# Opening stage of a two-block kernel: filter sizes summed on VectorE, the modulation bias added as columns, filter products on both halves of the array, the next stage's first operands requested early

## The reference, cut to what matters

```
sh1, sc1, gt1, sh2, sc2, gt2 = split(silu_c @ ada_w + ada_b, 6)
hid  = sin(freq * (feats @ w1 + b1))
hid  = sin(freq * (hid @ w2 + b2))
filt = (hid @ w3) * exp(-t * deltas)
filt = filt / sum(abs(filt), axis=0)
return filt[:, :512], filt[:, 512:]
```

## Time and profile before

| | us |
|---|---|
| median of three runs (4322.47 to 4328.15) | 4327.37 |
| the profiled execution, its own time | 4322.88 |
| its span in the trace | 4321.1 |
| first stage, from the start to ScalarE's last instruction | 121.5 |
| second stage, VectorE's first instruction | 121.89 |
| TensorE busy over the span | 3857.2 (89%) |

### The profile page before, as it was taken

One profiled execution on the slowest core, in us unless ns is written; L12 is line 12 of the kernel. 1 busy time (PEld: TensorE's weight loads), 2 busy tenths in 40 slices (PEclk: granted clock), 3 DMA queues, 4 the chain that ended last, 5 costly groups with the idle time before them and its releaser, 6 DMA issues. The chain is left out here.

```text
span 4321.1 us, 97371 instructions
## 1 busy us (share of the span) xinstructions
PE 3857.2 (89%) x42381; PEld 2473.7 (57%) x42381; DVE 1430.2 (33%) x2510; ACT 1018.9 (24%) x2384; POOL 605.5 (14%) x748
## 2 busy tenths in 40 slices
PE   8798999998999969999979898978888799996995
PEld 2343446885444448888855444447777644445774
DVE  2556312133112220000023566545555522212003
ACT  2200100022011112222224343024544311112333
POOL 1020000001100000000010000235556311000112
PEclk8899999999999979999989999989999999998997
DMA  6261302003112169999982001100000121115998
GB/s 243 103 215 64 128 25 73 29 10 54 51 34 74 54 226 385 389 398 398 397 303 85 11 6 34 39 15 5 4 4 4 37 74 51 64 64 209 390 388 313
DMA packets 233430, 588.78 MB, mean 136 GB/s; under 512 B 36456, under 2 KB 140807, under 8 KB 213224
## 3 DMA queue, kind: packets, MB, share of 16 engines
q1 hardware_dynamic: 192291, 462.88, 29.3%
q0 software_dynamic: 19120, 73.68, 5.0%
q10 hardware_dynamic: 21782, 48.74, 3.3%
HBM read 514.20 MB, written 71.05 MB: 135 GB/s over the span
## 5 line engine op out<-in xcount | busy, mean ns | idle before, releaser
L1663 PE MATMUL experts_bank<-experts_uT,ex_wu 128*64 128x96 f32 x9216 | 390.0, 247 | 26.7 <-PE experts_bank L1649 22.4
L1663 PEld LDWEIGHTS experts_bank<-experts_uT,ex_wu 128*64 128x64 f32 x9216 | 383.7, 137 | 43.4 <-issue 43.4
L1736 DVE TENSOR_TENSOR experts_hT<-experts_si,experts_bank 128x384 f32<-128x384 f32 (+1 forms) x68 | 31.3, 460 | 724.8 <-PE experts_bank L1663 724.8
L192 PE MATMUL vgproj_bank<-vg_w,mix_hT 128*128 128x256 f32 x1024 | 225.6, 383 | 11.1 <-DVEq L201 7.6
L192 PEld LDWEIGHTS vgproj_bank<-vg_w,mix_hT 128*128 128x128 f32 x1024 | 195.6, 192 | 41.5 <-DVEq L201 8.4
L1663 PE MATMUL experts_bank<-experts_uT,b2z_hT 128*64 128x96 f32 x4096 | 178.7, 249 | 25.9 <-DMA b2z_hT<-in_w 11.9
L1663 PEld LDWEIGHTS experts_bank<-experts_uT,b2z_hT 128*64 128x64 f32 x4096 | 174.1, 138 | 39.6 <-issue 39.1
L1649 PE MATMUL experts_bank<-mixed_T,experts_hT 128*32 128x256 f32 (+1 forms) x2592 | 193.9, 451 | 0.0
L1691 ACT ACTIVATE experts_uT<-experts_bank,all_modrun 128x96 f32<-128x96 f32 x296 | 99.3, 439 | 218.8 <-PE experts_bank L1644 218.8
L1649 PEld LDWEIGHTS experts_bank<-mixed_T,experts_hT 128*32 128x32 f32 x2592 | 110.4, 110 | 69.6
L2286 POOL TENSOR_TENSOR b2z_hT<-b2z_hT,rwkv_level 128x256 f32<-128x256 f32 x192 | 140.7, 765 | 44.7 <-DVE b2z_hT L2765 34.7
(11 more groups left out here) (584 smaller groups left out, 6937.2 us busy)
## 6 DMA issues: line engine op xcount, KB each, us to landing
ex_wu<-in_expert_w SPq DMA_DIRECT2D x72, 2048.0 KB, 17.7
mixed_T<-in_expert_w SPq DMA_DIRECT2D x36, 2048.0 KB, 22.4
b2z_hT<-in_w SPq DMA_DIRECT2D x64, 1024.0 KB
b2z_Z<-in_w SPq DMA_DIRECT2D x32, 1024.0 KB, 12.1
keep_rows<-mix_hyT ACTq DMA_DIRECT2D x27, 768.0 KB, 8.8
keep_rows<-experts_yo ACTq DMA_DIRECT2D x68, 288.0 KB
mix_hT<-in_ada_w POOLq DMA_DIRECT2D x8, 2048.0 KB, 9.7
merge_w<-in_w_in SPq DMA_DIRECT2D x32, 512.0 KB, 6.0
```

The source lines that it names most:

```text
L192: last = pe.matmul(bk[t][:, 0:width], xT[:, k, t * P:(t + 1) * P], wt[:, s, k, :], start=(k == 0), stop=(k == KT - 1))
L1663: last = pe.matmul(bk[2 + j][c:c + 64, h * BT:(h + 1) * BT], wu[:, s, j, k, h * P + c:h * P + c + 64], uT[:, s, k, :], start=(k == 0), sto ...
```

## The change

- `norm_sum` runs once in place of eight times. VectorE adds the absolute values of the eight tiles up in `rn` (`heap`, seven additions of 128 x 1024), and TensorE sums that heap over positions behind piece 8.
- The bias row stays only for the four pieces of `SPREADS`. For the other eight the bias is added by VectorE at the end, as columns that `K.cols` already holds. The four turns of the `SPREADS` pieces into columns are gone, since only their spread form is used.
- `hid`, `w2`, `w3` and the vectors stand on both halves of the partitions. Of each tile's two filter products one uses rows 0 to 63 of the array, the other rows 64 to 127. This needs three more small transfers before `layered` is full (7 in place of 4), one more 256 KB transfer for `w3`, and two of 4 KB for `brow` in place of one of 24 KB.
- VectorE scales `fl` by `rn` at the end of the first stage and no longer in the second.
- SyncE requests three token tiles and two tables in the first stage, behind piece 9, into tiles that now live outside of both stages.

```diff
@@ phase_front, sync
+            sp.wait_ge(ada_mm, ada_item(9) + 1)
+            for n in range(3):
+                sp.dma_start(F.x[:, n, :], src[n * P:(n + 1) * P, :]).then_inc(F.xin[n], 16)
+                if n < 2:
+                    sp.dma_start(*fwd_table(I, F, n)).then_inc(F.full[n], 16)
@@ gpsimd
-            gp.wait_ge(layered, 64)
+            gp.wait_ge(layered, 112)
@@ tensor
-                pe.matmul(adab[i % 2][0:32, :], one2[:, :], brow[:, n * HALF:(n + 1) * HALF], start=False, stop=True).then_inc(ada_mm, 1)
+                if n in SPREADS:
+                    last = pe.matmul(adab[i % 2][0:32, :], one2[:, :], brow[:, SPREADS.index(n), :], start=False, stop=True)
+                last.then_inc(ada_mm, 1)
...
             def ada_turn(n):
                 pe.wait_ge(ada_out, ada_item(n) + 1)
+                if n in SPREADS:
+                    i = ada_item(n, spread=True)
+                    pe.wait_ge(ada_out, i - 1)
+                    pe.matmul(adab[i % 2][:, :], adasum[:, 2:2 + P], arow[:, n % 3, :], start=True, stop=True).then_inc(ada_mm, 1)
+                    return
...
-            def norm_sum(t):
-                pe.wait_ge(abss, t + 1)
+            def norm_sum():
+                pe.wait_ge(heaped, NT - 1)
                 for x in range(2):
-                    last = pe.matmul(sumb[x][:, :], K.ones[:, :], ab[:, t % 2, x * C:(x + 1) * C], start=(t == 0), stop=(t == NT - 1))
+                    last = pe.matmul(sumb[x][:, :], K.ones[:, :], rn[:, x * C:(x + 1) * C], start=True, stop=True)
                 last.then_inc(sums, 1)
             def filt(t):
...
-                    pe.matmul(fm[i % 3][:, :], hid[:, t * P:(t + 1) * P], w3[:, x * C:(x + 1) * C], start=True, stop=True).then_inc(mm, 1)
-                if t >= 1:
-                    norm_sum(t - 1)
+                    h = slice(64 * x, 64 * x + 64)
+                    pe.matmul(fm[i % 3][:, :], hid[h, t * P:(t + 1) * P], w3[h, x * C:(x + 1) * C], start=True, stop=True).then_inc(mm, 1)
@@ scalar
                 act.wait_ge(fls, 2 * t + 2)
-                if t >= 2:
-                    act.wait_ge(sums, t - 1)
-                act.activation(ab[:, t % 2, :], fl[:, t, :], ACT.Abs).then_inc(abss, 1)
+                if t >= 3:
+                    act.wait_ge(heaped, t - 2)
+                act.activation(ab[:, t % 2, :] if t else rn[:, :], fl[:, t, :], ACT.Abs).then_inc(abss, 1)
@@ vector
+            def heap(t):
+                dve.wait_ge(abss, t + 1)
+                if t >= 2:
+                    dve.wait_ge(heaped, t - 1)
+                dve.tensor_tensor(rn[:, :], rn[:, :], ab[:, t % 2, :], ALU.add).then_inc(heaped, 1)
...
+                if t >= 2:
+                    heap(t - 1)
+            heap(NT - 1)
+            dve.wait_ge(sums, 1)
             for x in range(2):
-                dve.reciprocal(rn[:, x * C:(x + 1) * C], sumb[x][:, :])
-            dve.wait_ge(ada_cols, ADA)
+                last = dve.reciprocal(rn[:, x * C:(x + 1) * C], sumb[x][:, :])
+            last.then_inc(summed, 1)
+            dve.wait_ge(summed, 1)
+            for t in range(NT):
+                dve.tensor_tensor(fl[:, t, :], fl[:, t, :], rn[:, :], ALU.mult)
+            dve.wait_ge(ada_cols, ADA - len(SPREADS))
...
@@ phase_forward_norm
-            tokens(0)
-            table(0)
-            tokens(1)
-            tokens(2)
-            table(1)
...
-                dve.tensor_tensor(fl[:, t, :], fl[:, t, :], rn[:, :], ALU.mult).then_inc(scaled, 1)
-                dve.wait_ge(scaled, t + 1)
                 dve.tensor_tensor(he[:, t, :], fl[:, t, 0:C], fl[:, t, C:2 * C], ALU.add).then_inc(hes, 1)
```

More of the change, by code:

```diff
@@ L592, in phase_front @@
         cc = m.sb("cc", [P, KT, 32])
-        brow = m.sb("brow", [1, 6 * D])
+        brow = m.sb("brow", [1, 4, HALF])
         one2 = m.sb("one2", [1, 32])
@@ L659, in ada_rows @@
                     for c in range(4):
[L660 to L662 removed]
+                        last = pe.matmul(adab[i % 2][32 * c:32 * c + 32, :], cc[:, 2 * c + q, :], ring[n % RING][:, 2 * c + q, :],
+                                         start=(q == 0), stop=(q == 1 and not (c == 0 and n in SPREADS)))
+                if n in SPREADS:
+                    last = pe.matmul(adab[i % 2][0:32, :], one2[:, :], brow[:, SPREADS.index(n), :], start=False, stop=True)
+                last.then_inc(ada_mm, 1)
             def ada_turn(n):
                 pe.wait_ge(ada_out, ada_item(n) + 1)
+                if n in SPREADS:
[3 more added lines that the diff above has]
+                    return
                 for q in range(4):
@@ L699, in _ @@
             pe.wait_ge(sine, 1)
-            pe.wait_ge(layered, 64)
+            pe.wait_ge(layered, 112)
             for x in range(2):
-                pe.matmul(fm[x][0:64, :], w2[:, :], hid[:, x * HALF:(x + 1) * HALF], start=True, stop=True).then_inc(lin, 1)
+                pe.matmul(fm[x][:, :], w2[:, :, :].rearrange("p a n -> p (a n)"), hid[0:64, x * HALF:(x + 1) * HALF], start=True, stop=True).then_inc(lin, 1)
             pe.wait_ge(silu_ok, 2)
             pe.wait_ge(zeroed, 6)
-            pe.wait_ge(browed, 16)
+            pe.wait_ge(browed, 32)
             ada_rows(0)
@@ L721, in _ @@
                 ada_turn(n - 1)
+                if n == 8:
+                    norm_sum()
             ada_turn(ADA - 1)
@@ L733, in _ @@
                 act.dma_start(*row_of(name, n)).then_inc(loaded, 16)
-            for to, what in ((w3[:, :], I["hy_ffn_w3"][0]), (negt[:, :], I["k_negt"]), (delta[:, :], I["k_delta"])):
+            for to, what in ((w3[0:64, :], I["hy_ffn_w3"][0]), (w3[64:P, :], I["hy_ffn_w3"][0]), (negt[:, :], I["k_negt"]), (delta[:, :], I["k_delta"])):
                 act.dma_start(to, what).then_inc(spread, 16)
-            act.dma_start(brow[:, :], I["ada_b"]).then_inc(browed, 16)
+            for x in range(2):
+                act.dma_start(brow[:, 2 * x:2 * x + 2, :].rearrange("a n k -> a (n k)"), I["ada_b"][:, (3 * x + 2) * D:(3 * x + 3) * D]).then_inc(browed, 16)
             def ada_evac(n):
                 act.wait_ge(ada_mm, ada_item(n) + 1)
-                if n >= 3:
-                    act.wait_ge(ada_cols, n - 2)
+                if n >= 3 and n - 3 not in SPREADS:
+                    act.wait_ge(ada_cols, sum(x not in SPREADS for x in range(n - 2)))
+                if n >= 3 and n - 3 in SPREADS:
+                    act.wait_ge(ada_mm, ada_item(n - 3, spread=True) + 1)
                 act.activation(arow[:, n % 3, :], adab[ada_item(n) % 2][:, :], ACT.Copy).then_inc(ada_out, 1)
@@ L765, in _ @@
             ada_evac(3)
-            act.wait_ge(spread, 48)
+            act.wait_ge(spread, 64)
             for t in range(NT):
@@ L807, in _ @@
                     dve.tensor_tensor(fl[:, t, x * C:(x + 1) * C], fm[i % 3][:, :], dec[:, t % 2, :], ALU.mult).then_inc(fls, 1)
-            dve.wait_ge(sums, NT)
+                if t >= 2:
+                    heap(t - 1)
+            heap(NT - 1)
+            dve.wait_ge(sums, 1)
             for x in range(2):
-                dve.reciprocal(rn[:, x * C:(x + 1) * C], sumb[x][:, :])
-            dve.wait_ge(ada_cols, ADA)
-            dve.wait_ge(cols_ok, 1)
-            then(dve.tensor_copy(ada[:, :, :].rearrange("p n j -> p (n j)"), cb[:, VGROUPS * P:VGROUPS * P + 96]))
+                last = dve.reciprocal(rn[:, x * C:(x + 1) * C], sumb[x][:, :])
[4 more added lines that the diff above has]
+            dve.wait_ge(ada_cols, ADA - len(SPREADS))
+            dve.wait_ge(cols_ok, 1)
+            at = PLACES["ada_b"][0]
+            cols = cb[:, VGROUPS * P:VGROUPS * P + 96].rearrange("p (n j) -> p n j", j=2)
+            for n in (0, 24):
+                last = dve.tensor_tensor(ada[:, n:n + 16, :], cols[:, n:n + 16, :],
+                                         K.cols[:, at + n:at + n + 16].rearrange("p (n a) -> p n a", a=1).to_broadcast([P, 16, 2]), ALU.add)
+            then(last)
             for out, vecname, sc, sh, j in ((0, "norm1_g", 1, 0, 0), (1, "norm1_g", 1, 0, 1), (2, "norm2_g", 4, 3, 0)):
@@ L834, in phase_forward_norm @@
         fb, nb = bk[0:FB], bk[FB:8]
-        full = m.sems("full0", "full1")
-        xin = m.sems(*[f"xin{n}" for n in range(XS)])
         evac = m.sems("evac0", "evac1")
-        scaled, hes, mm, copied, outs = m.sems("scaled", "hes", "mm", "copied", "outs")
+        hes, mm, copied, outs = m.sems("hes", "mm", "copied", "outs")
         summed, rooted, inv, yok, turned = m.sems("summed", "rooted", "inv", "yok", "turned")
```

64 lines of the change are left out of this document (33 added, 31 removed).

## The result

The changed kernel takes 4293.51 us (median of 4 runs, 4291.35 to 4294.65) against 4324.92 (4 runs) on the same chip: a ratio of 0.9928, 95% interval 0.9914 to 0.9942. It was measured twice more, beside the experiments: 0.9932 (0.9919 to 0.9945) and 0.9930 (0.9910 to 0.9950). The medians lie 31.4, 31.6 and 30.6 us under those of before; forecast were 4295 us, and 30.6 less. The profiled execution took 4294.09 us, with a span of 4292.3. As in the part ahead, L numbers are those of the kernel that the row is from.

A forecast was written before the change was run, and what follows sets the result against it. The prediction took TensorE to bound the filter-tile stretch and the 2 MB transfers the opening. First stage -23.3 and second stage -7.3 made -30.6 us, giving 4296.8, stated as 4295 us, range 4283 to 4311.

The forecast's parts named there:

- (1) The opening: First stage's start: three more small transfers delay GpSimd's first request by 1.9 us; first `dec` moves from 40.76 to 41.7.
- the whole slack that was worked out: In the opening: piece 0 may start as late as 24.0 instead of 19.26 without cost, 4.7 us.
- (2) The loop: First stage's filter tiles: ScalarE and VectorE bind at 29.0 us; last `abs` ends at 70.7, last addition at 72.0.
- the round of ScalarE and VectorE: In the loop: `dec`, two products and `abs` take 3.18 us per tile; eight tiles with copies between them 29.0.
- The rival that they don't: In the loop: row halves do not work side by side; gain only 20 to 24 us, about 4303; chance 0.10.
- One sign of a right prediction: In the loop: TensorE would be idle between filter tiles, waiting for VectorE.
- (3) The tail: First stage's end: VectorE's sum, reciprocals, scalings and small operations take 19.5 us, ending at 91.5 and hiding TensorE's last pieces.
- the signs of a wrong prediction: Loop clock below 0.7, a tile still 2 us, a wait for piece 11, or ScalarE's gates ending behind VectorE.
- (4) The lower clock: First stage: TensorE at the lower level for 36% as before, adding 6.1 us in the loop and 0.6 in the tail.
- the first rival: TensorE low through most of the loop; all low, it ends 17 us later, gain 12 to 16, about 4310; chance 0.15.
- The second stage: Its opening: TensorE starts 5.0 us sooner and the 2.3 us wait before its second group goes, together -7.3 us.
- The sum: Whole kernel: -23.3 us in the first stage and -7.3 in the second make -30.6.

The follow-up runs named there:

- one half: Both filter products of a tile on rows 0 to 63 of the array, against the changed kernel; run twice, ratios to the kernel before 0.9948 and 0.9950.
- the first profile: The changed kernel, unaltered, in its first profiled execution: 4294.09 us; ratio of its runs to the kernel before 0.9928.
- the third profile: The changed kernel run a third time, with no edit: ratio to the kernel before 0.9930.
- the first profile of before: The kernel before the change, unaltered, in its first profile; median of its runs 4324.92 us.
- the second profile of before: The kernel before the change run once more, with no edit: ratio 0.9998.
- sums on TensorE: Sums of absolute values back on TensorE, tile by tile, without VectorE's heap, against the changed kernel; ratio to the kernel before 0.9963.
- requests late: Token tiles and tables requested at the start of the second stage again, against the changed kernel; ratio to the kernel before 0.9937.
- scaling second: The eight scalings back in the second stage, against the changed kernel; ratio to the kernel before 0.9924.
- thin bias products: A bias-row product for every piece again, zero weights where the changed kernel has none, against the changed kernel; ratio to the kernel before 0.9942.
- six scalings: Both opening waits loosened and only six of eight scalings in the first stage, against the changed kernel; ratio to the kernel before 0.9924.

## Why the prediction was right, point by point

**(1) The opening.** GpSimd's first request at 8.0 was 8.40; piece 3 at 36.2 came at 37.2 to 37.5; the first `dec` at 41.7 came at 43.11, 41.36 and 41.93, mean 42.1. The bias row, put at about 22, came at 24.0, which used up the whole slack that was worked out. It cost nothing, as moving its wait showed. What the three transfers cost, 1.9 by the sum, was 1.6 to 2.4 at piece 3, and 1.9 and 2.4 at the `dec` where piece 3 took 3.64 us in both kernels. The sum was too small at piece 3 by about 1.0 to 1.3 all the same: with the request back at 6.25 piece 3 still starts at 35.6, and not at 34.25 as before. What holds it there no run shows.

**(2) The loop.** That the round of ScalarE and VectorE is the bound at full clock held in the main: at clock 1.00 VectorE waited for `dec` in seven tiles of eight (for TensorE's product, 2.52 us, in one, the third) and the loop took 27.57, with 29.0 forecast. The term was 1.4 too large, since the two products take 1.29 in the loop and not the 1.37 of tile 0, and a round without a copy is 3.03, not 3.18. The halves, taken as 1.0 us a tile, were 1.13. The upper bound of TensorE's work, 32 us on one half, was 28.9: the first three products need no bank to come free and are begun before the first `dec` (41.58 against 42.65 in the first run on one half), where the sum had all sixteen in the loop. The Trainium skill, TensorEngine Tiling (Array Packing), Key Properties, says that different tiles load and multiply in parallel, and the trace agrees for row halves too (1.13 against 1.98). The rival that they don't fell. One sign of a right prediction hardly shows, TensorE idle between filter tiles: its rows fill 28.6 of the loop's 29.1 us, with the waits for a bank inside them.

**(3) The tail.** 19.5 us from the last heap to VectorE's end was 20.2 in the first profile (73.57 to 93.80): reciprocals as said, scalings 9.2 and not 9.8, and from the heap to the reciprocals 3.7 us and not 2.0, at the lower clock (2.1 in the third profile, at full clock). VectorE was last in the first two profiles. In the third it was ScalarE's gate copy behind TensorE by 1.5 us, through the wait for piece 11, which stood among the signs of a wrong prediction. Piece 11 was to land 8.4 us behind its request, and before or nearly before the early requests; where TensorE waited for it, it took 10.2 to 10.6 us, and 15.6 in the third profile, with the early requests in its way.

**(4) The lower clock** was mis-sized, in its share and not in its price. I took the share of before, 36%, worth 6.1 us in the loop; the eight loops with both halves and the sums on VectorE took 27.6, 27.6, 29.1, 29.1, 30.6, 33.3, 33.9 and 34.0, which is 0 to 6.4 over the shortest and 3.1 in the mean. The share was 22% in the mean. Each microsecond at the lower level cost the loop 0.43 to 0.47 us, and the forecast had 0.48 (6.1 for 36% of 35 us). The second stage began 24.7 to 28.0 us earlier than in the first profile of before, for 23.3 forecast, the difference being this term and that of the round, less some 0.4 in the opening; the second profile of before is 2.0 later still. That TensorE would stand low through most of the loop, the first rival, did not happen in any of them.

**The second stage** was forecast at -7.3: from its first operation to g3 it is 19.88 before and 12.61 after, -7.27. But with the scaling simply left in the second stage only 2.8 would be lost, so that most of this is work moved: VectorE's 9.2 us of scaling stand in the first stage's tail instead, as the sum had them. The early requests (3.5) belong in the sum by themselves. The forecast did not split them.

**The sum**, -30.6 for the profiled execution and the medians alike, met the medians to within 1 us, and that is in part luck. At g3 it is 4.7 short of the mean (-35.3), since the lower clock and the round were put too high; that the medians keep only some 31 of it was in no term, and what takes the rest is not resolved.

**Which edit does what**, each undone alone, at g3: sums on TensorE +8.7, one half +3.6 and +7.5 (of it 1.3 to 1.8 the halves at a given clock), requests late +3.5 from the stage's start, scaling second +2.8 from the reciprocals, thin bias products +2.9 (of it 2.0 to 2.2 in the opening, the rest within the clock's scatter). They don't add up to 35, as each is measured with the others in place: once TensorE is under the round of 27.6 us, what is taken off it frees nothing more at full clock. No edit was made alone on the kernel of before, where TensorE was busy throughout the loop and the halves may have been worth more.

## What to carry to other kernels

When an engine is taken off a loop's critical path, work out the round of the engines that remain: it caps what the next relief is worth, and here the sums moved to VectorE (8.7 us, with the other edits in place) brought more than any other edit. Where the clock makes a stage scatter by more than an edit's size, compare at equal clock or count from a mark behind the loop, since the edits worth 2 to 4 us (early requests, six scalings) could be read in no ratio. A long wait within a full stream of transfers, like the 4.5 us for the bias row, may cost nothing, while the request that starts the stream costs what it is late (2.15 us at the request, 1.9 at the first `dec`). And early requests share the engines with what is still landing: they gained 3.5 us here and in one run cost 1.5.

## What the runs showed of the hardware that was not expected

The lower clock came in blocks of several microseconds, some of them behind stretches in which TensorE was busy without a gap. Windows of the kernel with the bias wait moved:

```profile
44.00:48.00 4.00, 4.00 (x28) 1.66 (x22) 1.29 (x2) 2.64 (x5) 0.88 (x1) 1.00 1.03 387
48.00:52.00 4.00, 4.00 (x12) 1.07 (x12) 2.51 (x4) 2.21 (x3) 0.00 (x0) 0.66 1.03 389
52.00:56.00 4.00, 4.00 (x17) 0.57 (x10) 2.33 (x3) 1.06 (x1) 0.00 (x0) 0.50 1.01 383
56.00:60.00 4.00, 4.00 (x6) 1.01 (x6) 0.00 (x0) 1.44 (x3) 0.88 (x1) 0.50 0.75 229
60.00:64.00 4.00, 4.00 (x21) 0.77 (x18) 2.42 (x3) 1.45 (x3) 0.00 (x0) 0.63 1.01 392
64.00:70.00 6.00, 5.89 (x27) 1.63 (x28) 3.18 (x5) 3.44 (x5) 0.88 (x1) 1.00 0.85 296
```

In eight loops with the same mixture of work the time at the lower level was 0 in two, and 3.5 to 13.6 us in the others (with two levels, twice the missing share of the clock times the length). One thing separates them: where piece 3, just ahead of the loop, ran at the lower level (3.32 to 3.64 us), the loop had 0.94 or 1.00, in four runs; where it ran at full clock (1.92) or partly so (2.77), the loop had 0.80 to 0.89, in the other four. The block at the lower level lay mostly ahead of the loop or mostly in it. The two runs on one half had a slow piece 3 (3.35 and 3.41) and a slow loop. "Busy without a gap" is also no proof of work without a pause, since a row can hide a wait for a bank, as the row of 47.65 to 51.70 us does in this run, in which the clock falls. What sets the lower clock off these runs don't tell.

The lower clock also makes the stream run dry: the DMA share falls to 0.75 while the slower engine holds the buffers (to 0.01 in 60 to 64 us in the second run on one half), so that the last pieces are requested later (piece 11 at 74.2 to 74.5 at clock 0.80, at 67.8 and 69.2 at 1.00).

The bias row, a small transfer, was there 11.8 us after its request was issued (12.2 to 24.0), while the DMA engines, with the weights' stream on them, stood at 1.03 busy (12 to 24 us).
